# Folding the even filter arrays a second time: half the rows for the even half of a 2048-point transform

## What is computed

```
h = (h @ w3).reshape(L, 2, HY_ORDER, D_HY) * exp(-t * deltas)
h_f, h_b = h[:, 0], h[:, 1]
h_full = concatenate([h_f, zeros, h_b[1:][::-1]])       # 2 L taps
h_full = h_full / (sum(abs(h_full)) + NORM_EPS)
return rfft(h_full, axis=0)                              # L = 1024 (and 128)
```

## Time and profile before

| | |
|---|---|
| time, median of 3 runs | 3781.95 us (3778.77 to 3788.82) |
| the profiled execution | 3784.86 us, its span 3783.2 us |
| mean granted TensorE clock | 0.945 of 2.4 GHz |
| busy, share of the span | TensorE 89%, its weight loads 83%, VectorE 48%, ScalarE 29%, GpSimd 21% |
| matmuls in the span | 18430 |
| moved by DMA | 524.36 MB, 139 GB/s in the mean |

### The profile page before, as it was taken

How to read it: one execution, slowest core, us unless ns; L and a number is a source line. 1 busy time by engine, 2 the same in 40 slices (tenths; PEclk the granted TensorE clock), 3 DMA queues, 4 the chain that set the end, 5 groups by cost and what they waited for, 6 DMA issues and landing times. The chain is left out here.

```text
span 3783.2 us, 48485 instructions
## 1 busy us (share of the span) xinstructions
PE 3379.1 (89%) x18430; PEld 3132.1 (83%) x18430; DVE 1828.5 (48%) x2323; ACT 1107.9 (29%) x1765; POOL 803.6 (21%) x393
## 2 busy tenths in 40 slices
PE   2788969999999999988898799999999999888889
PEld 1566669798889999976788798888989999866889
DVE  7645533345445474257543231544543762377351
ACT  2343443244334212122112232443443111122111
POOL 3222113112211111222122221221121111112123
PEclk6688989999999999999999899999999999999999
DMA  6444342344333343365443433433423434466434
GB/s 205 148 134 128 122 161 91 115 117 124 95 104 100 130 166 132 126 217 199 163 146 133 153 131 117 119 102 100 129 90 116 155 138 142 158 207 204 147 115 167
DMA packets 210548, 524.36 MB, mean 139 GB/s; under 512 B 36388, under 2 KB 84133, under 8 KB 208966
## 3 DMA queue, kind: packets, MB, share of 16 engines
q1 hardware_dynamic: 203430, 496.28, 39.6%
q10 hardware_dynamic: 6912, 25.17, 2.5%
HBM read 392.69 MB, written 155.73 MB: 145 GB/s over the span
## 5 line engine op out<-in xcount | busy, mean ns | idle before, releaser
L2087 PE MATMUL ps<-hh,w_high 128*128 128x384 f32 x1152 | 414.0, 359 | 5.4 <-ACT attn_fout L2238 4.4
L2087 PE MATMUL ps<-hh,w_low 128*128 128x384 f32 x1152 | 394.4, 342 | 0.0
L2087 PE MATMUL ps<-hl,w_high 128*128 128x384 f32 x1152 | 392.9, 341 | 0.0
L1308 PE MATMUL ps<-hh,w_high 128*128 128x384 f32 x1344 | 310.3, 338 | 7.2 <-PEq L116 7.2
L1308 PE MATMUL ps<-hl,w_high 128*128 128x384 f32 x1344 | 306.5, 335 | 0.0
L1308 PE MATMUL ps<-hh,w_low 128*128 128x384 f32 x1344 | 306.3, 335 | 0.0
L2397 DVE TENSOR_REDUCE attn_nmax<-ps 128x1 f32<-128x1280 f32 x144 | 195.4, 1357 | 149.4 <-PE ps L2110 149.3
L2417 DVE TENSOR_TENSOR attn_wl<-ps,attn_wh 128x512 fp32r<-128x512 f32 (+2 forms) x200 | 117.4, 587 | 290.4 <-ACT attn_wh L2274 290.4
L1308 PEld LDWEIGHTS ps<-hh,w_high 128*128 128x128 f32 x1344 | 239.9, 188 | 11.6 <-POOLq L1407 7.8
L2264 ACT ACTIVATE low<-ps,attn_nmax 128x1280 f32<-128x1280 f32 x144 | 176.4, 1225 | 231.7 <-DVE attn_nmax L2397 231.7
L1308 PEld LDWEIGHTS ps<-hl,w_high 128*128 128x128 f32 x1344 | 240.6, 189 | 0.0
(11 more groups left out here) (291 smaller groups left out, 7584.3 us busy)
## 6 DMA issues: line engine op xcount, KB each, us to landing
tables<-in_dft_conv SPq DMA_DIRECT2D x64, 512.0 KB, 4.2
gates<-attn_fout SPq DMA_DIRECT2D x144, 192.0 KB, 2.2
branch_gate<-gates SPq DMA_DIRECT2D x48, 576.0 KB, 4.0
w_raw<-in_w_mg ACTq DMA_DIRECT2D x48, 512.0 KB, 4.1
mixin_grow<-in_w_ada SPq DMA_DIRECT2D x48, 512.0 KB, 3.7
conv_dh<-tables SPq DMA_DIRECT2D x96, 256.0 KB, 2.9
conv_dl<-tables SPq DMA_DIRECT2D x96, 256.0 KB, 3.7
aux<-qk SPq DMA_DIRECT2D x64, 288.0 KB, 6.1
```

Source lines behind the costliest of these rows:

```text
L1308: last = pe.matmul(dst, w[:, b, k, :], x[:, k, cols], start=(k == 0 and n == 0), stop=(k == KD - 1 and n == 2))
L2087: last = pe.matmul(ps[:, X_BANK, 0:CH], w[:, j % 2, k, :], x[:, k, (c % 3) * CH:(c % 3 + 1) * CH], start=(k == 0 and n == 0), stop=(k == K ...
```

## The change

Folds `f` = 0 and 2 are folded once more about their own middle, 512 samples into two times 256. Of the cosine fold the sum serves the frequencies 4q and the difference 4q + 2; of the sine fold the difference serves 4q and the sum 4q + 2. The first fold goes into a new buffer `once` (in the freed `araw`), the two halves go side by side into the same 512 columns of `fold`, and the rows of the even matrices are cut to 256 (or padded with zeros where the host still stores 512): `rows_of` names the two blocks that a tile uses. An even tile thus loads, casts, subtracts and multiplies 2 blocks instead of 4, and multiplies 6 times instead of 12; the two matmuls with the middle row stay in tiles 0, 2 and 16 and go in 4 and 6. Odd tiles stay as they are. The middle sample of the fold takes the place of sample 512 in `both`, with a semaphore `quarter` for its turn. The stores, the casts of the folds and the order of all steps stay.

```
...
                  "zero", "both", "fold", "tr", "evh", "evl", "l1", "inv", "invst", "dh", "dl", "H", "hout", "st0", "st1",
                  "din0", "din1", "ain0", "ain1", "ain2", "ada", "scond", "cst", "hpm", "hpo", "hpst", "w2z", "x", "cond",
-                 "xsq", "xadd", "ssm")
+                 "xsq", "xadd", "ssm", "quarter")
         S = {n: ph.sem(n) for n in names}
...
         xs = (both[:, 2, 1], taps[:, 0, 0], taps[:, 0, 1], taps[:, 1, 0], taps[:, 1, 1], spare, taps[:, 0, 0], taps[:, 0, 1])
         condb = both[:, 3, :, 0:D_MODEL]
+        once = [araw[:].rearrange("p a n -> p (a n)")[:, 3 * BR + i * (FOLD + 1):3 * BR + (i + 1) * (FOLD + 1)] for i in range(2)]
         waste = hout[:].rearrange("p a n -> p (a n)")
...
             n, r = divmod(q, 4 * CT)
             return (n, r // 2, 2 * (r % 2)) if r < 2 * CT else (n, (r - 2 * CT) // 2, 1 + 2 * (r % 2))
+        def rows_of(t):
+            if 8 <= t < 16:
+                return tuple(range(NK))
+            return (0, 1) if t in (0, 1, 2, 3, 16) else (2, 3)
...
                     if m >= 2:
                         sp.wait_ge(S["dl"], m - 1)
-                    sp.dma_start(draw[:, m % 2], A["dft_taps"][F_ORDER[m % NS]]).then_inc(s_din[m % 2], 16)
+                    t = F_ORDER[m % NS]
+                    n = len(rows_of(t))
+                    sp.dma_start(draw[:, m % 2, 0:n], A["dft_taps"][t][:, 0:n]).then_inc(s_din[m % 2], 16)
...
                     else:
                         pe.wait_ge(S["both"], 2 * (n * CT + ct) + 2)
+                        pe.wait_ge(S["quarter"], n * CT + ct + 1)
                     if g >= 2:
...
                         pe.wait_ge(S["hout"], m - 1)
                     arr = ((0, 2), (1, 3))[8 <= t < 16][t % 2]
-                    mid_row = arr == 0
+                    rows = rows_of(t)
+                    mid_row = t in (0, 2, 16)
                     bank = ps[:, m % 2, :]
                     if mid_row:
                         pe.matmul(bank, sgn[:], mid[:], start=True, stop=False)
-                    for k in range(NK):
+                    for k, row in enumerate(rows):
                         for i, (w, x) in enumerate(((dh, xh), (dh, xl), (dl, xh))):
-                            last = pe.matmul(bank, w[:, m % 3, k, :], x[:, arr, k, :],
-                                             start=(not mid_row and k == 0 and i == 0), stop=(k == NK - 1 and i == 2))
+                            last = pe.matmul(bank, w[:, m % 3, k, :], x[:, arr, row, :],
+                                             start=(not mid_row and k == 0 and i == 0),
+                                             stop=(k == len(rows) - 1 and i == 2))
                     last.then_inc(S["H"], 1)
...
                     buf, src = fold[:, q % 4], both[:, ct, f // 2, :]
                     near, far = slice(1, FOLD), slice(TS - 1, FOLD, -1)
-                    if f < 2:
-                        dve.tensor_copy(buf[:, 0:1], src[:, 0:1]).then_inc(S["fold"], 1)
-                    elif f == 2:
-                        dve.memset(buf[:, 0:1], 0.0).then_inc(S["fold"], 1)
+                    if f in (1, 3):
+                        dve.tensor_copy(buf[:, 0:1], src[:, (0, FOLD)[f // 2]:(0, FOLD)[f // 2] + 1]).then_inc(S["fold"], 1)
+                        dve.tensor_tensor(buf[:, 1:], src[:, near], src[:, far], ALU.add if f == 3 else ALU.subtract
+                                          ).then_inc(S["fold"], 1)
+                        return
+                    e = once[f // 2]
+                    if ct or n:
+                        p, c = divmod(n * CT + ct - 1, CT)
+                        dve.wait_ge(S["fold"], 2 * folded(p, c, f) + 2)
+                        if f == 0:
+                            dve.wait_ge(S["quarter"], n * CT + ct)
+                    if f == 0:
+                        chain(dve.tensor_copy(e[:, 0:FOLD + 1:FOLD], src[:, 0:FOLD + 1:FOLD]))
+                        chain(dve.tensor_tensor(e[:, 1:FOLD], src[:, near], src[:, far], ALU.add))
+                        dve.tensor_copy(src[:, FOLD:FOLD + 1], e[:, FOLD // 2:FOLD // 2 + 1]).then_inc(S["quarter"], 1)
                     else:
-                        dve.tensor_copy(buf[:, 0:1], src[:, FOLD:FOLD + 1]).then_inc(S["fold"], 1)
-                    dve.tensor_tensor(buf[:, 1:], src[:, near], src[:, far], ALU.add if f in (0, 3) else ALU.subtract
-                                      ).then_inc(S["fold"], 1)
+                        chain(dve.tensor_tensor(e[:, 1:FOLD], src[:, near], src[:, far], ALU.subtract))
+                        chain(dve.tensor_copy(e[:, FOLD:FOLD + 1], e[:, FOLD // 2:FOLD // 2 + 1]))
+                    for i, op in enumerate((ALU.add, ALU.subtract) if f == 0 else (ALU.subtract, ALU.add)):
+                        dve.tensor_tensor(buf[:, i * FOLD // 2:(i + 1) * FOLD // 2], e[:, 0:FOLD // 2], e[:, FOLD:FOLD // 2:-1], op
+                                          ).then_inc(S["fold"], 1)
...
                     if m >= 3:
                         dve.wait_ge(S["H"], m - 2)
-                    dve.tensor_tensor(dl[:, m % 3], draw[:, m % 2], dh[:, m % 3].bitcast(F32), ALU.subtract
+                    k = len(rows_of(F_ORDER[m % NS]))
+                    dve.tensor_tensor(dl[:, m % 3, 0:k], draw[:, m % 2, 0:k], dh[:, m % 3, 0:k].bitcast(F32), ALU.subtract
                                       ).then_inc(S["dl"], 1)
...
                 for i in range(14, NA):
                     modulation(i)
+                dve.wait_ge(S["ada"], 2 * NA)
+                chain(dve.memset(once[1][:, 0:1], 0.0))
                 for ct in range(CT):
...
                     if m >= 3:
                         act.wait_ge(S["H"], m - 2)
-                    nc.scalar.copy(dh[:, m % 3], draw[:, m % 2]).then_inc(S["dh"], 1)
+                    k = len(rows_of(F_ORDER[m % NS]))
+                    nc.scalar.copy(dh[:, m % 3, 0:k], draw[:, m % 2, 0:k]).then_inc(S["dh"], 1)
...
             forward[e, kind] = _quarters(_transform(TS, kind, k, n + 0.5), e == 0)
             m = _transform(TS, kind, _frequencies(TS, e, kind, False), n)
-            if e == 1 and kind == "s":
-                m[0] = _transform(TS, "s", _frequencies(TS, 1, "s", False), [FOLD])[0]
+            if kind == "s":
+                m[0] = _transform(TS, "s", _frequencies(TS, e, "s", False), [FOLD // (2 - e)])[0]
+            if e == 0:
+                m[FOLD // 2:] = 0
             tiles["t" + kind] = _rows_by_tile(m)
...
     k = _frequencies(TS, 0, "c", False)
     k[0] = TS
-    taps.append(_rows_by_tile(_transform(TS, "c", k, n))[0])
+    taps.append(_rows_by_tile(_transform(TS, "c", k, n) * (n < FOLD // 2)[:, None])[0])
     C["dft_taps"] = np.stack(taps)
...
```

## The result

The changed kernel takes 3751.64 us (median of 4 runs, 3749.78 to 3757.57), the kernel before, beside it on the same chip, 3783.37 us: a ratio of 0.9918, 95% interval 0.990 to 0.9936. The forecast was 3769, range 3754 to 3785. The profiled execution took 3753.14 us, with a span of 3751.5 against 3783.2: 31.7 us less, where the sum had 13.3.

A forecast was written before the change was run, and what follows sets the result against it. It took a closed ring of spectrum copy, store, next matrix load, landing and cast, without TensorE, to bound the filter stage; -3.3 - 23.0 + 7.8 + 5.2 = -13.3 us gave 3769 us, range 3754 to 3785.

The forecast's parts named there:

- the sum: Filter stage, all terms together: -3.3 - 23.0 + 7.8 + 5.2 = -13.3 us, taken over unchanged to the whole kernel.
- The first paragraph's step: Filter stage runs alone and ends in a barrier, so each microsecond won or lost at its end is one of the total.
- Products: TensorE in the filter stage: 216 matmuls fewer, nearly all off the path except at the first two spectra; -3.3 us.
- Loads and casts: Even matrix tiles in the filter stage: half-size loads and casts save 0.72 us in each of 32 steps; -23.0 us.
- the landing: Even matrix tiles, from the load's issue to the cast, 2.85 us: 0.5 us shorter with 128 KB instead of 256.
- The count: Filter stage: 32 steps gain from smaller loads and casts, 5 in unit 0 and 9 in each later unit.
- Folds: VectorE's added folds in the filter stage: +7.8 us before the first spectrum and +5.2 us inside units 0 to 2.
- The landing did shrink: Rival on the filter stage's matrix loads: landing hardly gets shorter, time between 3777 and 3785 us; chance 0.17.
- TensorE was on the path: Rival in the filter stage: all 49.7 us of saved matmuls count, 3740 us, or added folds hide, 3755; chance 0.10.
- The folds beside GpSimd: Rival in the filter units: added VectorE folds held by POOL's operations cost 25.8 instead of 5.2 us, 3789 us; chance 0.08.
- The rival on the clock: Rival in the filter stage: TensorE, with less to do, stays at 1.2 GHz, 24 us over 32 odd steps, 3793; chance 0.05.
- the terms' bounds: Filter stage, best and worst values: products 0 to -4.5, loads and casts -7.0 to -31.0, prologue +4.0 to +9, units 0 to +13.

The follow-up runs named there:

- b_pe80: The kernel before with 80 instructions that do nothing added to TensorE's stream, ahead of the later stages: 0.55% faster than the kernel before.
- a_pe176: The changed kernel with 176 instructions that do nothing added to TensorE's stream, ahead of the later stages: 3773.11 us.
- a_fill: The changed kernel with 128 do-nothing TensorE instructions ahead of the later stages and 8 unused matmuls before each attention head's first scores: 3752.15 us, ratio 0.9904.
- a_pe128: The changed kernel with 128 instructions that do nothing added to TensorE's stream, ahead of the later stages: 3767.36 us.
- b_halfmm: The kernel before with half of the even arrays' products left out and 176 do-nothing TensorE instructions added: 3776.91 us, ratio 0.9981.
- a_casts: The changed kernel with loads of the even arrays' tiles at full 256 KB and their casts at all four rows again: 3771.62 us, ratio 0.9958.

## Why the prediction was wrong

- **The first paragraph's step failed**: "a microsecond won or lost at its end is one of the total". It took the later stages' time as given because their instructions don't change. TensorE's stream got 448 instructions shorter ahead of them, and their time fell by 20.7 us, 12.5 of them in attention, the others within what the remaining stages differ by from execution to execution. A shorter stream moved the loop of attention against the blocks in which code comes, that cut an idle stretch in two, and TensorE's clock stayed up. b_pe80 gives this part without the change, a_pe176 takes it from the change, a_fill gives it without the place. Without it the changed kernel would stand near a_pe176's 3773.11 or a_pe128's 3767.36, which is what the sum forecast (3769).
- **The stage's sum held, its terms less so.** 13.3 us were forecast and 11.0 came. Part of that is luck: the terms measured one by one give 5.0, and each is known to some 5 us only. Products: 3.3 forecast, 6 to 7 measured, 2.4 of them before the first hout (139.69 in b_halfmm against 142.11). Loads and casts: 23.0 forecast, 14.4 measured. The size for one step was about right: the landing is 0.46 us shorter (2.81 to 2.35; 0.5 was taken from the pair of the earlier trace rows), and the steps of unit 3 are as forecast (3.62 in the median, 3.66). The count was not: six of the 32 steps are among the twelve behind a load of `decay`, and from a_casts, with full loads and casts, to the changed kernel they gain 0.1 us each (62.3 to 61.7 together); the other 26 gain 0.60 (114.5 to 98.9), where 0.72 was forecast. The rule of the Trainium skill (DMA: Bandwidth & Descriptors, section Anatomy of one DMA), by which 128 KB less is an estimated 0.30 us, comes out low here for one landing. Folds: 13.0 forecast, 15.4 measured, 7.4 of them before the first hout (7.8 forecast).
- **The rivals.** The landing did shrink. TensorE was on the path by some 6 us, not by 49.7. The folds beside GpSimd cost what was put on them. The rival on the clock had the sign wrong, and the stage: the clock decided, outside the filters, and for faster.
- **The range** was made from the terms' bounds alone. None of its cases had a term for stages that the change doesn't touch.

## What to carry to other kernels

A change that adds or removes instructions ahead of a loop moves that loop's code for its engine: before a gain is put down to the work, give the old kernel the new instruction count, and see whether the stages that weren't edited move. Where an engine waits for a load, look at what the load's issue waits for: here two lines in SyncE's order brought the stage's end further forward than the whole change, and only with them did halving TensorE's products pay, in the unit that folds nothing for a next one. An idle stretch of TensorE costs more than its length if the clock falls after it, and work without use in it can be worth its time.

## What was not expected of the hardware

- 80 instructions without effect made an unchanged kernel 0.55% faster (interval 0.32% to 0.78%), and eight useless matmuls a head won 0.5% (0.9904 against 0.9955).
- A wait for one piece of code at a loop's jump (1.3 to 1.9 us) did no harm and some good: about the same idle time in one piece of 2.8 to 3.1 us was followed by 14 to 18 matmuls of 128x384 at 1.2 GHz.
- Waits that were long met didn't delay TensorE inside the running loop: 14 of them, 0.106 us each where they stood by themselves, added 1.5 us in the first head of a layer only.
